# The first expert's token numbers from a one-column product, and what is queued behind its gathered rows

## The chip, the cores and the metric

One core of a Trainium2 chip runs the whole kernel in one launch. The metric is device time in microseconds (us), of one execution; the median of three runs stands for the kernel.

## The reference, cut to what matters

The kernel computes one step of a one-layer hybrid encoder over 576 tokens (512 of a prompt, 64 of a running stream) of 1024 features: a pooling mixer and a gated linear attention, a first layer norm that gives h, and then a routed mixture of experts on h with a second layer norm.

```python
logits = jnp.dot(x2, w_router) + b_router            # x2 = h, 576 x 1024; 32 experts
top_val, top_idx = lax.top_k(logits, TOP_K)          # 4 experts per token
gates = jax.nn.softmax(top_val, axis=-1)
...
gu = jnp.dot(xb, w_gu[e]) + b_gu[e]                  # xb: the rows of h routed to expert e
gate, up = gu[:, :EXPERT_FF], gu[:, EXPERT_FF:]
gate = jnp.minimum(gate, SWIGLU_LIMIT)
up = jnp.clip(up, -SWIGLU_LIMIT, SWIGLU_LIMIT)
hmid = gate * jax.nn.sigmoid(SWIGLU_ALPHA * gate) * (up + 1.0)
return jnp.dot(hmid, w_down[e]) + b_down[e]
...
y = _layer_norm(alpha * h + moe_out, ln2_g, ln2_b)
```

Each expert holds 12.6 MB of float32 weights: w_gu (8.4 MB) and w_down (4.2 MB). All 32 are read once.

## The kernel before, in words

The kernel is written by hand, one instruction list per engine, with counting semaphores between them; there is no planner. Each engine does its list in the order of the text.

**Two stages.** The first (some 228 us) makes h in five token tiles (four of 128 tokens, one of 64), stores h to DRAM from ACT's queue (L882), and routes each tile. The second loops over 32 experts, up to 96 tokens each.

**The weights.** `load(e, i, s)` (L515) brings piece i of expert e, 2 MB, into slot s of a ring of 8 slots in SBUF: pieces 0 to 3 are w_gu, 4 and 5 are w_down, below written (e, i). SP issues all of them in order. Ahead of the experts it issues (0,0) to (0,3), (1,0) and (1,1); then, after `mix_ready`, (0,4) and (0,5); then the gate and up biases (L532) once h is stored; then it waits for `gathered[0]`, the landing of expert 0's rows, and goes on with (1,2) and all others. Piece (e, i) waits for `split_done`, which says that the piece that was in its slot eight pieces earlier has been converted; piece (e, 1), whose slot held (e-2, 5), waits instead for `down_read`, the end of the last matmul of expert e-2. So (1,2) needs expert 0's pairs 0 and 1, and (2,1) needs the end of expert 0.

**The float16 pairs.** Float32 weights are multiplied as a high and a low half in float16. A piece is two "pairs" of 128 x 2048. For pair p of expert n, ACT writes the high half (`next_hi`, L871) and DVE the low one (`next_lo`, L1835, counted by `split_done`); PE multiplies both against the tokens' high and low halves. Pairs 0 to 3 are gate and up of the first half, 4 to 7 of the second, 8 and 9 the first half of w_down; the rest of w_down goes in float32. The four buffers come free by `unit_used`.

**Which tokens.** `rank` holds for every token its place in each expert. DVE's `onehot(m, e)` (L1765) compares the places with 0..127 and gives five 128 x 128 matrices `hot`. PE's `table(m, e)` multiplies them with `info`, four columns per expert: gate high, gate low, slot number, token number. DVE's `rows_of` copies the result to `found` (L1775) and makes the integer token numbers `tok_i` (L1777); POOL's `gather` (L684) then fetches those rows of h by an indirect DMA into `xg`. PE transposes them (`rows`, L1316), ACT and DVE make the halves (`rows_hi` L895, `rows_lo` L1826). A small product, `sel_ready`, picks the 96 slots out of 128, and `places_of` (L1783 to L1790) turns them into the scatter's addresses. The `table` product of expert 1 also counts the tokens of all experts, in float32.

**The seam between the stages.** For the last tile DVE does `route(4)` (the top four), then `gate_info(4)` (L1667 to L1674: softmax and the columns of `info`), `rank_tile(4)` (L1681), then `onehot(0)`, `rows_of(0)`, `onehot(1)`, `rows_of(1)`, two constants, the matrices `used` and `used16` (L1849 to L1852), the biases (L1853, `bias_ready`), `next_lo(0,0)`, `next_lo(0,1)`, `rows_lo(0)`, `places_of(0)`, `next_lo(0,2)` and on. PE fills its waits with products that nobody reads (`idle(n)`: n matmuls of 512 columns); they keep it active. POOL, after the last `pow` (L665), waits for all states and h rows to be stored, clears `xg` (L670), writes two index tables (L672, L674) that only the overflow loop reads, and gathers.

The queue order in SP's list around the change (L527 to L533):

```python
sp.wait_ge(mix_ready, TILES)
for i in (4, 5):
    load(0, i, piece_slot(0, i))
sp.wait_ge(hT_ready, 2 * TILES)
sp.wait_ge(h_stored, 16 * TILES)
sp.dma_start(bguT[:, 0:E, :], b_gu).then_inc(late_in, 16)
sp.wait_ge(gathered[0], 16)
```

Of the kernel before, what the change touches and what calls it, by code (L numbers as in the profile page):

```python
# [26 lines left out]
ALU = mybir.AluOpType  # L27
# [3 lines left out]
P = 128  # L31
# [4 lines left out]
TILES = 5  # L36
# [15 lines left out]
E = 32  # L52
TOPK = 4
FF = 1024
BLK = 96
# [18 lines left out]
def build(nc, x_prompt, x_sample, x_t, state_pool, state_gla, w_in, w_glr, w_pool, pool_scale, w_gate_up,  # L74
# [3 lines left out]
    with ExitStack() as ctx:  # L78
# [261 lines left out]
        acc_out, ln2_in = sem("acc_out"), sem("ln2_in")  # L340
# [127 lines left out]
        def _(sp):  # L468
# [58 lines left out]
            sp.wait_ge(mix_ready, TILES)  # L527
            for i in (4, 5):
                load(0, i, piece_slot(0, i))
            sp.wait_ge(hT_ready, 2 * TILES)  # L530
            sp.wait_ge(h_stored, 16 * TILES)
            sp.dma_start(bguT[:, 0:E, :], b_gu).then_inc(late_in, 16)  # L532
            sp.wait_ge(gathered[0], 16)  # L533
            for e in range(1, E):
                for i in range(2 if e == 1 else 0, PER):

                    if e == 2 and i == 0:
                        sp.dma_start(bd, b_down[0]).then_inc(bd_in, 16)
# [48 lines left out]
        def _(pool):  # L587
# [74 lines left out]
            for t in range(TILES):  # L662
# [4 lines left out]
            pool.wait_ge(states_out, 96)  # L667
            pool.wait_ge(h_stored, 16 * TILES)
            pool.wait_ge(mix_ready, TILES)
            step(pool.memset(xg, 0.0))  # L670
            pool.wait_ge(zeroed, 32)
            pool.iota(val_e, pattern=[[1, E], [0, MAXB - 1]], base=0, channel_multiplier=0,  # L672
                      allow_small_or_imprecise_dtypes=True).then_inc(made, 1)
            pool.iota(val_b, pattern=[[0, E], [BLK, MAXB - 1]], base=BLK, channel_multiplier=0,  # L674
                      allow_small_or_imprecise_dtypes=True).then_inc(made, 1)
# [25 lines left out]
            gather(0, 0, 0)  # L701
            gather(1, 1, 1)
# [302 lines left out]
        def _(pe):  # L1005
# [278 lines left out]
            idle(8)  # L1284

            def table(m, e):

                pe.wait_ge(hot_ready, m + 1)
# [13 lines left out]

            def rows(m, q, got, tables):
# [6 lines left out]
                mm(bank[0][0:BLK, 484:488], used16, found[m % ROW_BUFS if isinstance(m, int) else 0], True, True)\  # L1310
                    .then_inc(sel_ready, 1)
                pe.wait_ge(gathered[q], got)
                for b in range(2):
# [4 lines left out]
                    last.then_inc(gT_ready, 1)  # L1318

# [54 lines left out]
            idle(12)  # L1374
# [76 lines left out]
        def _(dve):  # L1451
# [208 lines left out]

            def gate_info(t):
# [7 lines left out]
                step(dve.tensor_tensor(each_g, each, g4.unsqueeze(2).to_broadcast([n, TOPK, E]), ALU.mult))  # L1669
                step(dve.tensor_reduce(gate, each_g.rearrange("p k e -> p e k"), AX.X, ALU.add))  # L1670
# [70 lines left out]
            dve.sem_inc(unit_used, BUFS)  # L1741
            route(TILES - 1)
            gate_info(TILES - 1)
            rank_tile(TILES - 1)
# [23 lines left out]
            def rows_of(m, q, last):  # L1768
# [4 lines left out]
                if isinstance(m, int) and m == 1:  # L1773
# [3 lines left out]
                dve.tensor_scalar(tok_i[q], found[q][:, 3:4], float(PLACES), None, ALU.add)\  # L1777
                   .then_inc(rows_known, 1)
# [69 lines left out]
            four = ident.rearrange("p (g d) -> p g d", d=4)  # L1848
            step(dve.tensor_copy(used[:, 0:BLK].rearrange("p (g d) -> p g d", d=3), four[:, :, 0:3]))  # L1849
            step(dve.tensor_copy(used[:, BLK:P].rearrange("p (g d) -> p g d", d=1), four[:, :, 3:4]))  # L1850
# [4 lines left out]
            next_lo(0, 0)  # L1855
            next_lo(0, 1)
            rows_lo(0, 0)
# [166 lines left out]
```

## Time and profile before

| | us |
|---|---|
| three runs, median (lowest to highest) | 1274.15 (1273.35 to 1274.99) |
| the profiled execution, own time | 1276.51 |
| its span in the profile | 1274.6 |
| PE busy | 1204.8 (95%) |
| DVE busy | 1050.7 (82%) |
| ACT busy | 945.0 (74%) |
| POOL busy | 176.3 (14%) |

Times in the rows below are microseconds from the start of the span, except where marked ns. PE is the matmul engine (TensorE), PEld its weight load, DVE VectorE, ACT ScalarE, POOL GpSimd, SP the engine that only issues DMAs; SPq and ACTq are their queues. A busy share is an average over stages: what a change in one stage is worth is read from that stage.

### The profile page before, as it was taken

The numbers are of one execution on the slowest core, as the hardware profiler recorded it, in microseconds if no ns is written. First come the engines' busy times: TensorE is split into PE (matmuls) and PEld (weight loads), VectorE is DVE, ScalarE is ACT, GpSimd is POOL, SyncE is SP. The second block draws the span as 40 slices with busy tenths as digits, with TensorE's granted clock in tenths as the row PEclk, the third lists the DMA queues.
The fourth block names the chain that finished last, engine by engine and source line by source line (L and its number), as shares of the span: only waits on it lengthen the run. The fifth ranks groups of instructions, "written<-read, shape, count | busy, mean of one in ns | idle before, by whom it ended". The sixth has DMA issues, their size and how long they took to land.

```text
span 1274.6 us, 35057 instructions
## 1 busy us (share of the span) xinstructions
PE 1204.8 (95%) x15390; PEld 872.2 (68%) x15390; DVE 1050.7 (82%) x1200; ACT 945.0 (74%) x1260; POOL 176.3 (14%) x145
## 2 busy tenths in 40 slices
PE   7999998799999999999999999999999999999985
PEld 3555555677777777777777777777777777777742
DVE  5565666899999889998988888888888888888877
ACT  5433311688989888988888888888888888888821
POOL 1264210111011100000000111111111111111002
PEclk9999997899999999999999999999999999999987
DMA  9562393599999999999999999999999999999982
GB/s 364 221 253 85 116 412 126 228 363 415 424 424 426 425 425 424 426 425 425 426 424 425 426 425 425 426 424 424 427 425 423 426 424 423 425 427 424 405 360 87
DMA packets 46839, 475.00 MB, mean 373 GB/s; under 512 B 8701, under 2 KB 9620, under 8 KB 20828
## 3 DMA queue, kind: packets, MB, share of 16 engines
q1 hardware_dynamic: 34636, 438.58, 82.2%
q0 software_dynamic: 11392, 31.77, 6.6%
q8 instruction: 124, 2.03, 0.6%
q10 hardware_dynamic: 656, 2.36, 0.5%
q14 instruction: 31, 0.25, 0.1%
HBM read 452.99 MB, written 29.95 MB: 379 GB/s over the span
## 4 chain that ended last, share of the span: by engine, by line
PE 34%; DMA 32%; DVE 9%; ACT 4%; issue 4%; DVEq 0%; ACTq 0%
PE wide L1007 23%; DMA ring<-in_w_gu 22%; PE bank L1007 9%; DMA ring<-in_w_down 8%; DVE work L1835 5%; ACT work L871 3%; DMA work<-part_rows 2%; PE bank L1316 1%; ACT work L901 1%; DVE ring L1967 1%; DVE ring L1965 1%; DVE work L1826 0%; DVE work L1765 0%; DVE ring L1954 0%; DVE work L1820 0%
## 5 line engine op out<-in xcount | busy, mean ns | idle before, releaser
L1835 DVE SCALAR_TENSOR_TENSOR work<-ring,work 128x2048 f16<-128x2048 f32 x320 | 721.3, 2287 | 109.7 <-ACT work L871 101.4
L871 ACT ACTIVATE work<-ring 128x2048 f16<-128x2048 f32 x320 | 599.6, 1902 | 93.9 <-DMA ring<-in_w_gu 67.1
L1007 PE MATMUL wide<-work 128*128 128x96 f16 (+2 forms) x7024 | 481.6, 229 | 34.6 <-issue 9.3
L1007 PEld LDWEIGHTS wide<-work 128*128 128x128 f16 (+2 forms) x7024 | 372.2, 101 | 129.0 <-issue 45.9
L1007 PEld LDWEIGHTS bank<-work 128*128 128x128 f16 (+4 forms) x6530 | 301.2, 101 | 39.7 <-issue 23.6
L1007 PE MATMUL wide<-ring,work 128*96 128x512 f32 (+3 forms) x1004 | 327.5, 493 | 0.0
L1007 PE MATMUL bank<-work 128*128 128x96 f16 (+4 forms) x6530 | 311.9, 208 | 9.2 <-DVE work L1765 3.6
L1007 PEld LDWEIGHTS wide<-ring,work 128*96 128x96 f32 (+3 forms) x1004 | 128.6, 134 | 172.7 <-issue 122.8
L684 POOL DMA_INDIRECT work<-h_rows,work x32 | 61.2, 1913 | 459.5 <-PE bank L1316 443.9
L697 POOL DMA_INDIRECT part_rows<-work x30 | 44.4, 1480 | 376.2 <-ACT work L931 376.2
L901 ACT ACTIVATE work<-wide,work 128x96 f32<-128x96 f32 x256 | 64.9, 333 | 0.0
L901 ACT ACTIVATE work<-bank,work 128x96 f32<-128x96 f32 x256 | 64.8, 333 | 0.0
L931 ACT ACTIVATE work<-wide,work 96x1024 f32<-96x1024 f32 x30 | 33.1, 1102 | 31.4 <-PE wide L1007 31.3
L910 ACT ACTIVATE work<-work 128x384 f32<-128x384 f32 x64 | 39.4, 616 | 2.1
L917 ACT ACTIVATE work<-work 128x384 f32<-128x384 f32 x64 | 39.4, 616 | 2.1
L863 ACT ACTIVATE work<-bank 128x512 f32<-128x512 f32 (+1 forms) x10 | 5.0, 553 | 44.5 <-PE bank L1234 44.5
L1815 DVE SCALAR_TENSOR_TENSOR work<-work 128x384 f32<-128x384 f32 x64 | 35.5, 555 | 1.3 <-DVE work L1805 0.2
L1458 DVE SCALAR_TENSOR_TENSOR ring<-ring 128x1024 f16<-128x1024 f32 x16 | 19.3, 1223 | 20.1 <-ACT ring L767 20.0
L1805 DVE SCALAR_TENSOR_TENSOR work<-work 128x384 f32<-128x384 f32 x64 | 35.2, 551 | 0.0
L1316 PE MATMUL bank<-work 128*128 128x128 f32 x256 | 34.5, 277 | 0.4 <-issue 0.4
L1826 DVE SCALAR_TENSOR_TENSOR work<-bank,work 128x384 f16<-128x384 f32 x64 | 32.5, 549 | 0.0
L895 ACT ACTIVATE work<-bank 128x384 f16<-128x384 f32 x64 | 27.3, 476 | 6.3 <-PE bank L1316 6.3
(205 smaller groups left out, 591.5 us busy)
## 6 DMA issues: line engine op xcount, KB each, us to landing
ring<-in_w_gu SPq DMA_DIRECT2D x128, 2048.0 KB, 30.1
ring<-in_w_down SPq DMA_DIRECT2D x64, 2048.0 KB, 33.2
part_rows<-work POOLq DMA_DIRECT2D x1, 10240.0 KB, 37.2
ring<-part_rows SPq DMA_DIRECT2D x3, 2560.0 KB, 27.5
ring<-in_w_in SPq DMA_DIRECT2D x3, 2048.0 KB, 13.2
ring<-in_w_out SPq DMA_DIRECT2D x2, 2048.0 KB, 10.5
h_rows<-work POOLq DMA_DIRECT2D x1, 2560.0 KB, 9.9
ring<-h_rows SPq DMA_DIRECT2D x1, 2560.0 KB, 23.2
```

The costliest lines, as they stand in the source:

```text
L684: pool.indirect_dma_start(xg, None, h_dram, bass.IndirectOffsetOnAxis(ap=tok_i[q], axis=0), bounds_check=PLACES - 1, oob_is_err=False)\
L697: pool.indirect_dma_start(part_dram, bass.IndirectOffsetOnAxis(ap=dst_i[p], axis=0), orow, None, bounds_check=TOPK * SPAN - 1, oob_is_err= ...
L871: act.activation(whi[buf(n, p)], packed(s, p), ACT.Copy, scale=W_UP).then_inc(hi_done, 1)
L901: last = act.activation(dst[:, c, :], b[:, c * BLK:(c + 1) * BLK], ACT.Relu, scale=-DOWN * S_UP, bias=bguT[:, at[0], at[1] + c:at[1] + c + 1])
L910: act.activation(sg, g1, ACT.Sigmoid, scale=-SWISH / S_UP, bias=sig_bias).then_inc(sig_done, 1)
L917: act.activation(u1, u1, ACT.Relu, scale=-1.0, bias=up_bias).then_inc(up_clip, 1)
L931: act.activation(orow, wide[1 if isinstance(n, int) else 0][0:BLK, :], ACT.Copy, scale=slots[p][:, 5:6])\
L1007: return pe.matmul(out, w, x, start=start, stop=stop, skip_group_check=True)
L1316: last = pe.transpose(bank[b][:, k * BLK:k * BLK + P], xg[:, (4 * b + k) * P:(4 * b + k + 1) * P], used)
L1805: dve.scalar_tensor_tensor(g1, g1, -LIMIT * S_UP, sg, ALU.add, ALU.mult).then_inc(gated, 1)
L1815: dve.scalar_tensor_tensor(hm[:, 4 * half:4 * half + 4, :], u1, (1.0 - LIMIT) * S_UP, g1, ALU.add, ALU.mult)\
L1835: dve.scalar_tensor_tensor(wlo[buf(n, p)], packed(s, p), W_UP, whi[buf(n, p)], ALU.mult, ALU.subtract).then_inc(split_done, 1)
```

## The change

It touches only the seam between the stages.

- SP: (0,4) and (0,5) are issued after the wait for `gathered[0]` instead of after `mix_ready`; the biases go ahead of them.
- POOL: `xg` is cleared as soon as `mix_ready` is there; the first gather waits for `h_stored` and its token numbers; the wait for the states and the two index tables come behind it.
- DVE: the two copies into `used` come ahead of `route(4)`. Then `first_hot` makes expert 0's one-hot matrices of tiles 0 to 3, `rank_tile(4)`, the fifth matrix, and `gate_info(4)`, in the midst of which `first_ids` turns the new product into token numbers. `onehot(0)` and the first `tok_i` of `rows_of` are gone. `next_lo(0,0)` comes ahead of the constants, `rows_lo(0)` ahead of `next_lo(0,1)`, and `used16` and the biases behind it.
- PE: after `positions(4)` three idle products instead of eight, then the one-column product (five matmuls, the token column of expert 0 alone), then four idle ones. Expert 0's select product goes behind the transposes and waits there for `bias_ready`. Twelve idle products ahead of `rows(0)` become six.

```diff
@@ SP
-            sp.wait_ge(mix_ready, TILES)
-            for i in (4, 5):
-                load(0, i, piece_slot(0, i))
             sp.wait_ge(hT_ready, 2 * TILES)
             sp.wait_ge(h_stored, 16 * TILES)
             sp.dma_start(bguT[:, 0:E, :], b_gu).then_inc(late_in, 16)
+            sp.wait_ge(mix_ready, TILES)
             sp.wait_ge(gathered[0], 16)
+            for i in (4, 5):
+                load(0, i, piece_slot(0, i))
@@ POOL
-            pool.wait_ge(states_out, 96)
-            pool.wait_ge(h_stored, 16 * TILES)
             pool.wait_ge(mix_ready, TILES)
             step(pool.memset(xg, 0.0))
-            pool.wait_ge(zeroed, 32)
-            pool.iota(val_e, ...)
-            pool.iota(val_b, ...)
+            pool.wait_ge(h_stored, 16 * TILES)
             gather(0, 0, 0)
+            pool.wait_ge(states_out, 96)
+            pool.wait_ge(zeroed, 32)
+            pool.iota(val_e, ...)
+            pool.iota(val_b, ...)
             gather(1, 1, 1)
@@ PE
             positions(TILES - 1)
-            idle(8)
+            idle(3)
+            pe.wait_ge(hot_ready, 1)
+            for t in range(TILES):
+                n = ROWS[t]
+                last = mm(bank[0][:, 488:489], hot[0:n, t, :], info[0:n, t, 0, 3:4], t == 0, t == TILES - 1)
+            last.then_inc(ids_ready, 1)
+            idle(4)
@@ PE, table
-                pe.wait_ge(hot_ready, m + 1)
+                pe.wait_ge(hot_ready, m + 2)
@@ PE, rows
                 if not isinstance(m, int) or m > 0:
                     pe.wait_ge(dst_known, m)
-                else:
-                    pe.wait_ge(bias_ready, 1)
-                mm(bank[0][0:BLK, 484:488], used16, found[...], True, True).then_inc(sel_ready, 1)
+                    select(m)
                 pe.wait_ge(gathered[q], got)
                 ... the eight transposes ...
+                if isinstance(m, int) and m == 0:
+                    pe.wait_ge(bias_ready, 1)
+                    select(m)
@@ PE
             table(0, 0)
             table(1, 1)
-            idle(12)
+            idle(6)
             rows(0, 0, 16, 2)
@@ DVE
+            def first_hot(tiles):
+                for t in tiles:
+                    n = ROWS[t]
+                    last = dve.tensor_scalar(hot[0:n, t, :], iota16[0:n, :], rank[0:n, t, 0:1], None, ALU.is_equal)
+                return last
+            def first_ids():
+                dve.wait_ge(ids_ready, 1)
+                dve.tensor_scalar(tok_i[0], bank[0][:, 488:489], float(PLACES), None, ALU.add).then_inc(rows_known, 1)
@@ DVE, gate_info, behind the product with the gates
+                if t + 1 == TILES:
+                    first_ids()
@@ DVE
+            step(dve.tensor_copy(used[:, 0:BLK]..., four[:, :, 0:3]))
+            step(dve.tensor_copy(used[:, BLK:P]..., four[:, :, 3:4]))
             route(TILES - 1)
+            first_hot(range(TILES - 1))
+            rank_tile(TILES - 1)
+            first_hot([TILES - 1]).then_inc(hot_ready, 1)
             gate_info(TILES - 1)
-            rank_tile(TILES - 1)
+            dve.nop().then_inc(hot_ready, 1)
@@ DVE, rows_of
+                if not isinstance(m, int) or m > 0:
                     dve.tensor_scalar(tok_i[q], ...).then_inc(rows_known, 1)
@@ DVE
-            onehot(0, 0)
             rows_of(0, 0, None)
             onehot(1, 1)
             rows_of(1, 1, None)
+            next_lo(0, 0)
             step(dve.memset(sig_bias, SWISH * LIMIT))
             step(dve.memset(up_bias, 2 * LIMIT * S_UP))
-            ... the two copies into used ...
+            rows_lo(0, 0)
+            next_lo(0, 1)
             dve.wait_ge(late_in, 16)
             step(dve.tensor_copy(used16, used[:, 0:BLK]))
             dve.tensor_scalar(bguT[:, 0:E, :], ...).then_inc(bias_ready, 1)
-            next_lo(0, 0)
-            next_lo(0, 1)
-            rows_lo(0, 0)
             places_of(0, 0)
             next_lo(0, 2)
```

## Rows read from the trace of the kernel before

**Rows 1.** The page's part 4, the chain that ended last, by engine.
```profile
PE 34%; DMA 32%; DVE 9%; ACT 4%; issue 4%; DVEq 0%; ACTq 0%
```

**Rows 2.** Busy time by stretch: PE, PEld, DVE, ACT, POOL, then PEclk, DMA share, GB/s.
```profile
240.00:271.00 31.00, 28.90 (x436) 22.79 (x437) 29.75 (x36) 25.64 (x33) 3.82 (x2) 1.00 0.94 359
271.00:274.00 3.00, 3.00 (x49) 2.17 (x48) 3.00 (x2) 1.11 (x1) 0.00 (x0) 1.00 0.56 135
274.00:277.00 3.00, 3.00 (x75) 3.00 (x73) 2.12 (x7) 2.54 (x2) 1.09 (x1) 1.00 0.85 333
277.00:1191.00 914.00, 888.29 (x13010) 685.65 (x13007) 803.76 (x828) 793.05 (x1015) 100.17 (x59) 1.00 1.01 425
```

**Rows 3.** Timeline of SP's queue: start, duration, instruction, count.
```profile
240.69 6.06 SPq L515 DMA_DIRECT2D ring<-in_w_gu  x2
...
272.28 0.80 SPq L515 DMA_DIRECT2D ring<-in_w_gu  x2
```

**Rows 4.** Timeline of DVE through the seam; in brackets idle time before, and releaser.
```profile
225.71 0.15 DVE L1667 RECIPROCAL work<-work 64x1 f32<-64x1 f32 x1 [0.35 <-ACT work L888]
...
226.48 0.37 DVE L1670 TENSOR_REDUCE work<-work 64x32 f32<-64x128 f32 x1
...
227.63 0.18 DVE L1681 SCALAR_TENSOR_TENSOR work<-wide,work 64x32 f32<-64x32 f32 x1
227.97 1.83 DVE L1765 TENSOR_SCALAR work<-work 128x128 f16<-128x128 f16 x5
...
230.45 0.15 DVE L1777 TENSOR_SCALAR work<-work 128x1 int32<-128x1 f16 x1
230.52 0.89 DVE L1765 TENSOR_SCALAR work<-work 128x128 f16<-128x128 f16 x5
...
234.73 0.15 DVE L1777 TENSOR_SCALAR work<-work 128x1 int32<-128x1 f16 x1
...
236.12 4.49 DVE L1835 SCALAR_TENSOR_TENSOR work<-ring,work 128x2048 f16<-128x2048 f32 x2
...
241.90 4.50 DVE L1835 SCALAR_TENSOR_TENSOR work<-ring,work 128x2048 f16<-128x2048 f32 x2
```

**Rows 5.** Timeline of PE through the seam.
```profile
229.86 0.36 PE L1007 MATMUL bank<-work 128*128 128x4 f16 x5 [2.31 <-DVE work L1765]
231.47 2.80 PE L1007 MATMUL bank<-work 128*128 128x32 f32 x15 [1.25 <-DVE work L1765]
234.20 4.12 PE L1007 MATMUL wide<-work 128*128 128x512 f16 x12
...
238.18 1.07 PE L1316 MATMUL bank<-work 128*128 128x128 f32 x8
241.59 8.52 PE L1007 MATMUL bank<-work 128*128 128x96 f16 x197 [2.34 <-DVE work L1826]
```

**Rows 6.** Timeline of POOL, and the first two gathers' times from issue to landing.
```profile
228.10 1.01 POOL L670 MEMSET work<- 128x1024 f32 x1 [8.90 <-issue]
...
231.49 1.18 POOL L684 DMA_INDIRECT work<-h_rows,work  x1 [1.23 <-DVE work L1777]
...
DMA to landing us min/median/max: 3.6/6.9/10.2
```

**Rows 7.** Timeline of ACT: rows' high halves, then the first pairs' that wait for PE.
```profile
238.85 0.93 ACT L895 ACTIVATE work<-bank 128x384 f16<-128x384 f32 x2 [6.33 <-PE bank L1316]
243.93 3.87 ACT L871 ACTIVATE work<-ring 128x2048 f16<-128x2048 f32 x2 [4.15 <-PE bank L1007]
```

**Rows 8.** Stretches with TensorE's granted clock; columns as in Rows 2.
```profile
226.70:230.10 3.40, 1.09 (x9) 0.42 (x7) 2.81 (x10) 3.37 (x4) 1.92 (x3) 1.00 0.33 88
230.10:237.00 6.90, 5.65 (x24) 3.63 (x24) 3.53 (x17) 2.42 (x2) 1.34 (x2) 0.51 0.17 48
```

**Rows 9.** Groups of instructions running between 294.3 and 295.1: count, busy us, mean ns.
```profile
L1835 DVE SCALAR_TENSOR_TENSOR work<-ring,work 128x2048 f16<-128x2048 f32 x1 | 2.3, 2286 | 0.0
...
L707 POOL IOTA work<- 96x580 f32 x1 | 0.7, 657 | 0.0
```

More of the change, by code:

```diff
@@ L339, in build @@
         ov_place = sem("ov_place")
-        acc_out, ln2_in = sem("acc_out"), sem("ln2_in")
+        ids_ready, ln2_in = sem("ids_ready"), sem("ln2_in")
         y_done, y_stored = sem("y_done"), sem("y_stored")
@@ L701, in _ @@
             gather(0, 0, 0)
+            pool.wait_ge(states_out, 96)
+            pool.wait_ge(zeroed, 32)
+            pool.iota(val_e, pattern=[[1, E], [0, MAXB - 1]], base=0, channel_multiplier=0,
+                      allow_small_or_imprecise_dtypes=True).then_inc(made, 1)
+            pool.iota(val_b, pattern=[[0, E], [BLK, MAXB - 1]], base=BLK, channel_multiplier=0,
+                      allow_small_or_imprecise_dtypes=True).then_inc(made, 1)
             gather(1, 1, 1)
@@ L1301, in table, with select @@
                 last.then_inc(table_ready, 1)
+            def select(m):
+                mm(bank[0][0:BLK, 484:488], used16, found[m % ROW_BUFS if isinstance(m, int) else 0], True, True)\
+                    .then_inc(sel_ready, 1)
             def rows(m, q, got, tables):
@@ L1307, in rows @@
                     pe.wait_ge(dst_known, m)
-                else:
-                    pe.wait_ge(bias_ready, 1)
-                mm(bank[0][0:BLK, 484:488], used16, found[m % ROW_BUFS if isinstance(m, int) else 0], True, True)\
-                    .then_inc(sel_ready, 1)
+                    select(m)
                 pe.wait_ge(gathered[q], got)
@@ L1741, in _ @@
             dve.sem_inc(unit_used, BUFS)
+            four = ident.rearrange("p (g d) -> p g d", d=4)
+            step(dve.tensor_copy(used[:, 0:BLK].rearrange("p (g d) -> p g d", d=3), four[:, :, 0:3]))
+            step(dve.tensor_copy(used[:, BLK:P].rearrange("p (g d) -> p g d", d=1), four[:, :, 3:4]))
             route(TILES - 1)
+            first_hot(range(TILES - 1))
+            rank_tile(TILES - 1)
+            first_hot([TILES - 1]).then_inc(hot_ready, 1)
             gate_info(TILES - 1)
-            rank_tile(TILES - 1)
+            dve.nop().then_inc(hot_ready, 1)
             def counts():
@@ L1776, in rows_of @@
                 dve.wait_ge(table_copied, m + 1)
-                dve.tensor_scalar(tok_i[q], found[q][:, 3:4], float(PLACES), None, ALU.add)\
-                   .then_inc(rows_known, 1)
+                if not isinstance(m, int) or m > 0:
+                    dve.tensor_scalar(tok_i[q], found[q][:, 3:4], float(PLACES), None, ALU.add)\
+                       .then_inc(rows_known, 1)
             def places_of(m, q):
@@ L1844, in _ @@
             rows_of(1, 1, None)
+            next_lo(0, 0)
             step(dve.memset(sig_bias, SWISH * LIMIT))
             step(dve.memset(up_bias, 2 * LIMIT * S_UP))
-            four = ident.rearrange("p (g d) -> p g d", d=4)
-            step(dve.tensor_copy(used[:, 0:BLK].rearrange("p (g d) -> p g d", d=3), four[:, :, 0:3]))
-            step(dve.tensor_copy(used[:, BLK:P].rearrange("p (g d) -> p g d", d=1), four[:, :, 3:4]))
+            rows_lo(0, 0)
+            next_lo(0, 1)
             dve.wait_ge(late_in, 16)
```

4 lines of the change are left out of this document (removed).

## The prediction

> **What bounds the kernel now.** I read the chain of waits first, and it misleads. It lays 34% of the span on PE and 32% on DMA [rows 1], as if two engines shared the bound. The busy times by stretch correct it: from 277 to 1191 us, 914 us, the DMA share is 1.01 and the rate 425 GB/s [rows 2], with no slack anywhere between. The chain follows a weight piece back to whatever released its issue; it does not see that the piece then stood in a full queue. So nearly all of the span is one stream of weights, and its end moves with the time at which it last ran dry. That place is in rows 2 as well: from 240 to 271 the share is 0.94 at 359 GB/s, from 271 to 274 it is 0.56 at 135 GB/s, and after that it never falls again. What ends the hole is the issue of (2,1) and (2,2) at 272.28 [rows 3]. (2,1) needs the last matmul of expert 0 (`down_read`), so **expert 0's end sets the restart of the stream, and the restart sets the end of the kernel**. The seam counts in two ways only: when expert 0 ends, and whether the pieces ahead of (2,1) are through by then.
>
> **Token numbers and gather.** Before, DVE does the gate columns (225.71 on), ranks tile 4 at 227.63, compares until 229.80, PE multiplies, and the numbers are there at 230.45 + 0.15 = 230.60 [rows 4]. After: DVE is free of `route(4)` at 225.36 (0.35 ahead of 225.71). Four compares take 0.72, by the 0.89 for five at 230.52; the rank step takes 227.97 - 227.63 = 0.34; the fifth compare 0.18: 226.60. The five one-column matmuls are seen by DVE 0.40 after they may start (an estimate: the table of 229.86 took 0.36 [rows 5]): 227.06. DVE meanwhile does the first three gate steps, 226.48 - 225.71 = 0.77, until 227.37, and adds: 227.52, **3.1 earlier**. The gather started 231.49 - 230.60 = 0.89 behind its numbers and landed 3.6 after its start [rows 6], at 235.1; after: 228.4 and 232.0. Its other wait, h stored, was over when POOL began at 228.10 [rows 6] with 4 MB beside that store; without them it is no later. The two copies into `used` go into DVE's wait for the last logits; if that cover were gone they would cost 0.4.
>
> **Expert 1's table.** The rest of the gates, 227.63 - 226.48 = 1.15, runs until 228.7, and expert 0's table is copied by 229.3. The compares for expert 1 then take 0.89, or up to 1.83 where POOL writes beside them: those at 227.97 ran beside the clearing and the index tables at 228.10 and took twice as long [rows 4, 6]. The two tables now start at 228.4 + 1.18 = 229.6, in the middle of the compares; I take 1.3, until 230.6. From the end of the compares (231.41) to the end of `rows_of(1)` (234.88) it was 3.47 [rows 4]: **234.1, 0.8 earlier**. Of the 3.1 the gather gains, 2.3 are spent, on the longer way of DVE.
>
> **To expert 0's start.** PE: the idle products start 234.20 - 231.47 = 2.73 behind the table [rows 5], at 233.4, and six at up to 0.43 (the 12 took 4.12 with the last at full clock) end at 236.0; the rows have been there since 232.0. Transposes then, and ACT begins 238.85 - 238.18 = 0.67 later [rows 5, 7] and hands DVE its first half at 237.15. DVE: `next_lo(0,0)` 2.2 (half of the 4.4 that two take from start to start), two constants 0.2, until 236.5; it waits for 237.15; `rows_lo` 0.93 to 238.1; `next_lo(0,1)` to 240.3; `used16` and biases 0.6 (half of the 236.12 - 234.88 = 1.24 that they, the constants and the copies took [rows 4]) to 240.9. Only here may PE take the select product and, behind it, expert 0's first matmul: 241.0 against 241.59 [rows 5]. DVE waits 0.4 for the select, spends 0.45 on the addresses (0.93 and 0.45 are what 241.90 - 236.12 = 5.78 leaves beside the 4.4) and starts `next_lo(0,2)` at 241.75 **against 241.90** [rows 4].
>
> From there DVE has no idle time until expert 0's last pairs, and its work is unchanged: expert 0 ends with DVE. Its end is therefore **0.15 earlier**, 272.1. The new wait on `bias_ready` on PE is what makes it so little: behind it stands all of expert 0, and ahead of it the whole second pair.
>
> **The stream ahead of (2,1).** 240 to 274 carried 31 x 0.359 + 3 x 0.135 = 11.5 MB [rows 2]. (0,4) and (0,5) add 4.2, so 15.7 MB less what of it is behind (2,1)'s issue, some 0.3: 15.4. At 425 GB/s that is 36.3 us. Issued at 232.1, with 1 to 1.5 until data flow, they are through at 269.7 to 270; at the 0.359 that the stretch had before, taken for the five old pieces alone, at 232.1 + 1 + 9.9 + 31 = 274. I take the first, nearer since two pieces always stand in the queue now. Then the stream is dry at (2,1) as before and follows expert 0's end. At the second it joins without a hole, at about the time (274.1 by the 277 less what 3 us at 333 GB/s had fallen short of 425) that the old one was at full rate: no loss. The step that I put at nothing, two pieces out of an idle stretch into a full one (9.9 us of transfer), is so covered by 8.6 us of earlier issue and by the hole. If expert 0 ended before 270, they would cost.
>
> **Sum.** -0.15 at expert 0's end, and -0.2 for a hole that gets a little shorter: -0.35. Against the profiled execution, 1276.51, that is 1276.2; it stands 2.4 above the median of 1274.15, and with the same difference the forecast is **1273.8**. What a measurement of this kernel can tell is about 0.2%, 2.5 us.
>
> **A rule against the change.** Beside an index table of POOL at 294.4 a low-half conversion of DVE took 2286 ns [rows 9], as those at 236.12 and 241.90 do without one [rows 4]. This bears on the clearing of `xg`, which now runs at 219.2, right after the last `pow` and beside h's last operation on DVE, which leads the chain; I cost it at nothing. The Trainium skill, "GPSIMD Engine Reference", section "Specifications", says that VectorE and GpSimd contend when the DVE instruction uses a two-port mode or has two SBUF inputs. By that rule the conversion should have been slowed too (both inputs are in SBUF), and h's last operation would be. The compares agree with it, the conversion does not.
>
> **Rivals.**
> 1. *The clock stays up.* PEclk falls near 230.1, after a stretch with PE busy 1.09 of 3.4, and is 0.51 until 237 [rows 8]: 1.2 in place of 2.4 GHz. After the change four idle products and a table stand in that stretch, some 1.7. If this holds 2.4 GHz, the table of expert 1 and six idle products take half: 1.2 less to `rows_of(1)` and 2.4 less to the transposes. Then DVE waits for nothing: 1.6 less at `next_lo(0,2)`, **1272.3**. Against it: 1.7 is still half idle.
> 2. *That, and the stream joins.* With expert 0's end at 270.4 and the pieces through at 270 to 271.5, the hole closes too, 1.2 more: **1271.0**. Needs both.
> 3. *The clock is down at expert 0's start; slower.* Between transposes and select, 237.1 to 241.0, PE now has nothing, 3.9 us against 2.3 before 241.59 [rows 5]; before 229.86 an idle 2.31 and 1.25 more went with the fall. Its place is the first pairs of expert 0. At 2.4 GHz PE needs 8.52/197 x 48 = 2.1 for a pair [rows 5], under DVE's 2.2; at 1.2 GHz 4.2. One slow pair (243.93 + 1.6) is hidden, as DVE comes to pair 4 only at 247. Two end at 249.6, ACT's conversion (1.9 each [rows 7]) at 251.5, and DVE wants it at 249.1: +2.4, and some more behind: **1276.8**. It decides if 1.2 GHz lasts past about 247. The Trainium skill, "TensorE: Matmul & The Clock Gate", section "What's actually happening", has the clock set by how busy PE has lately been; by it both this and rival 1 are open.
> 4. *The port rule holds for h's last operation:* it grows by up to 1.0, the length of the clearing [rows 6], and all behind it: +1.0, **1274.8**.
> 5. *The gather lands no earlier* (indirect DMA issue or h's store late). Up to 236.0 the stream is through by 274.1 and nothing changes; behind that each us costs one.
>
> **How the numbers follow.** My forecast 0.46, rival 1 0.17, rival 2 0.13, rival 3 0.14, rivals 4 and 5 0.10. Faster by over 0.2% are rival 2 and a tail of rival 1: 0.17. Slower are rival 3 and a tail of 4 and 5: 0.15. The range takes in rivals 1 and 4, most of 2, the bounds of the idle products and of the compares (0.5 each), and goes to just short of rival 3, with 0.8 for the scatter of the runs: 1271.2 to 1276.5.
>
> **What the profile would show.** `tok_i` near 227.5, the gather at 228.4 and landing by 232; `rows_of(1)` done near 234.1; PE's first 96-column matmul near 241.0 behind a gap of nearly 4 us; `next_lo(0,2)` within 0.3 of 241.9; SP's (2,1) within 0.5 of 272.3 with a dip in the rate there; then 425 GB/s to the end. It is wrong if PEclk is 1.0 over 230 to 237 or 0.5 behind 243, if h is done later, or if the dip at 272 is gone.

## The result and the profile after

| | before | after |
|---|---|---|
| median, 20 runs each (lowest to highest), us | 1274.2 (1271.3 to 1277.4) | 1278.35 (1274.6 to 1281.1) |
| ratio, 95% interval | | 1.0032 (1.0023 to 1.0042) |
| the profiled execution: own time, span | 1276.51, 1274.6 | 1274.57, 1272.7 |
| mean granted clock, share of 2.4 GHz | 0.984 (138 runs) | 0.981 (20 runs) |

The changed kernel is slower by 4.1 us, above my range (1271.2 to 1276.5). The profiled execution of after is its shortest, that of before lies above its median, so the two spans stand the wrong way round. They must be compared from a common mark. I take the end of `route(4)` on DVE: 225.36 before (0.35 ahead of 225.71 [rows 4]), 222.17 + 0.37 = 222.54 after. It falls anywhere between 222.0 and 226.0 in the profiles below, whichever kernel they are of.

One part of the change lies ahead of this mark and costs 0.4 us there, which no number counted from the mark holds: the two copies into `used`. DVE before, then after, from the rank step of the tile ahead:

```profile
222.60 0.19 DVE L1681 SCALAR_TENSOR_TENSOR work<-bank,work 128x32 f32<-128x32 f32 x1
223.46 0.18 DVE L1649 TENSOR_TENSOR work<-bank,work 64x32 f32<-64x32 f32 x1 [0.66 <-PE bank L1007]
```

```profile
219.36 0.19 DVE L1708 SCALAR_TENSOR_TENSOR work<-bank,work 128x32 f32<-128x32 f32 x1
220.17 0.21 DVE L1771 COPY work<-work 128x96 f32<-128x96 f32 x1 [0.61 <-DVE work L1708]
...
220.64 0.18 DVE L1662 TENSOR_TENSOR work<-bank,work 64x32 f32<-64x32 f32 x1
```

The copies start only behind the idle 0.61 that was to cover them. From the end of the rank step to the mark it is 225.36 - 222.79 = 2.57 before and 222.54 - 219.55 = 2.99 after; it is 2.98 to 3.08 in all twelve profiles with the copies there and 2.52 to 2.93 in the six without.

The seam on DVE after (start, duration, instruction; in brackets idle time ahead of it and its releaser), answering to rows 4:

```profile
222.17 0.37 DVE L1671 TENSOR_REDUCE work<-work 64x32 f32<-64x128 f32 x1
...
224.48 0.16 DVE L1684 TENSOR_SCALAR work<-bank 128x1 int32<-128x1 f32 x1
...
226.37 1.60 DVE L1799 TENSOR_SCALAR work<-work 128x128 f16<-128x128 f16 x5
...
231.28 0.15 DVE L1812 TENSOR_SCALAR work<-work 128x1 int32<-128x1 f16 x1
231.37 2.29 DVE L1870 SCALAR_TENSOR_TENSOR work<-ring,work 128x2048 f16<-128x2048 f32 x1
...
234.96 1.02 DVE L1861 SCALAR_TENSOR_TENSOR work<-bank,work 128x384 f16<-128x384 f32 x2 [1.15 <-ACT work L896]
...
239.55 4.49 DVE L1870 SCALAR_TENSOR_TENSOR work<-ring,work 128x2048 f16<-128x2048 f32 x2
...
247.71 2.29 DVE L1870 SCALAR_TENSOR_TENSOR work<-ring,work 128x2048 f16<-128x2048 f32 x1 [0.43 <-ACT work L872]
...
251.08 4.49 DVE L1870 SCALAR_TENSOR_TENSOR work<-ring,work 128x2048 f16<-128x2048 f32 x2 [0.61 <-ACT work L872]
```

POOL's clearing and gather (answering to rows 6):

```profile
215.91 0.94 POOL L669 MEMSET work<- 128x1024 f32 x1
225.61 1.17 POOL L679 DMA_INDIRECT work<-h_rows,work  x1 [8.75 <-DVE work L1684]
```

PE (rows 5), then ACT (rows 7):

```profile
228.02 2.80 PE L1008 MATMUL bank<-work 128*128 128x32 f32 x15 [1.89 <-DVE work L1799]
230.75 2.74 PE L1008 MATMUL wide<-work 128*128 128x512 f16 x6
233.29 1.48 PE L1326 MATMUL bank<-work 128*128 128x128 f32 x8
238.82 11.17 PE L1008 MATMUL bank<-work 128*96 128x4 f16 x198 [4.05 <-DVE work L1886]
```

```profile
234.37 0.93 ACT L896 ACTIVATE work<-bank 128x384 f16<-128x384 f32 x2 [5.09 <-PE bank L1326]
243.04 1.91 ACT L872 ACTIVATE work<-ring 128x2048 f16<-128x2048 f32 x1 [7.75 <-PE bank L1008]
245.76 1.91 ACT L872 ACTIVATE work<-ring 128x2048 f16<-128x2048 f32 x1 [0.81 <-PE bank L1008]
```

What the change meant to do, it did: the gather starts 3.07 behind the end of `route(4)`, against 6.13. But PE stands idle for 4.05 us ahead of expert 0, and then its first 198 matmuls take 11.17 us, where 197 took 8.52 [rows 5]. The stretches show why (columns as in rows 2; after the comma PE busy, and the third number from the right is PEclk). After:

```profile
234.00:237.40 3.40, 0.77 (x6) 0.53 (x4) 2.44 (x3) 0.93 (x2) 1.04 (x1) 0.97 1.04 443
237.40:240.80 3.40, 1.98 (x25) 1.98 (x26) 3.00 (x8) 0.00 (x0) 0.00 (x0) 0.53 0.95 407
240.80:244.20 3.40, 3.40 (x46) 3.40 (x44) 3.40 (x4) 1.16 (x1) 0.00 (x0) 0.50 1.05 440
244.20:247.60 3.40, 3.40 (x81) 3.40 (x79) 2.94 (x6) 2.59 (x3) 0.00 (x0) 0.97 1.00 424
```

Before, over its first pairs:

```profile
238.20:241.60 3.40, 1.06 (x11) 0.82 (x9) 3.40 (x5) 0.93 (x2) 1.38 (x1) 1.00 0.00 0
241.60:245.00 3.40, 3.40 (x80) 3.40 (x81) 3.37 (x6) 1.07 (x1) 0.00 (x0) 1.00 0.98 323
```

After a stretch in which PE worked 0.77 of 3.4 us the clock fell to 1.2 GHz, near 237.6, and it came back near 244.4; 46 matmuls went through where before 80 did. ACT's conversions for pairs 4 and 5 wait for PE to free a buffer (7.75 and 0.81), and DVE waits for ACT (0.43, 0.61). Expert 0 ends late, and the stream restarts late. SP's queue and the stretches around the restart (rows 3 and 2):

```profile
229.46 0.81 SPq L515 DMA_DIRECT2D ring<-in_w_down  x2
238.21 6.20 SPq L515 DMA_DIRECT2D ring<-in_w_gu  x2
```

```profile
271.38 2.65 SPq L515 DMA_DIRECT2D ring<-in_w_gu  x3
```

```profile
268.00:271.00 3.00, 3.00 (x8) 1.08 (x7) 3.00 (x2) 1.50 (x1) 0.00 (x0) 1.00 0.59 243
271.00:274.00 3.00, 3.00 (x68) 2.81 (x67) 3.00 (x5) 1.62 (x2) 0.59 (x1) 1.00 0.61 153
274.00:277.00 3.00, 3.00 (x75) 3.00 (x73) 2.13 (x5) 2.93 (x2) 0.51 (x1) 1.00 0.97 415
277.00:1189.00 912.00, 886.34 (x12983) 684.31 (x12980) 803.13 (x828) 790.44 (x1014) 92.64 (x59) 1.00 1.01 424
```

From the end of `route(4)` to the issue of (2,1): 272.28 - 225.36 = 46.9 before, 271.38 - 222.54 = 48.8 after, **1.9 later**. The hole in the stream now takes in two of these stretches, and behind it the rate is 424 GB/s to the end (425 before).

The end of the kernel has a clock of its own. Its last stage, behind the stream, ends with 44 float32 products; before, then after (timeline of PE):

```profile
1246.39 15.78 PE L1007 MATMUL wide<-work 116*116 116x512 f32 x44 [1.98 <-DMA work<-part_rows]
```

```profile
1246.14 14.09 PE L1008 MATMUL wide<-work 116*116 116x512 f32 x44 [1.54 <-DMA work<-part_rows]
```

From the mark they start at 1021.03 before and at 1023.60 after, 2.6 us later, and with the 0.4 ahead of the mark 3.0. Then they take 1.7 less, with a mean granted clock of 0.87 behind 1240 against 0.80. No edit touches that stage, and b_swap (14.09) and b_swap2 (15.78), one and the same kernel, differ in the same way: it is luck, and it hides 1.7 us of the loss in this pair of profiles.

### The profile page after: what moved, and what is told of

The parts are those of the page before. It is cut to its first block, busy times and chain, and to the rows that moved or that the text cites. A ratio compares the mean times of both kernels' runs of the same rounds, so it can differ in the third digit from the quotient of the medians.

```text
span 1272.7 us, 35055 instructions
## 1 busy us (share of the span) xinstructions
PE 1202.8 (95%) x15388; PEld 874.0 (69%) x15388; DVE 1051.0 (83%) x1200; ACT 944.2 (74%) x1260; POOL 168.0 (13%) x145
## 4 chain that ended last, share of the span: by engine, by line
PE 57%; DMA 24%; DVE 10%; ACT 4%; issue 4%; POOL 0%; DVEq 0%; SPq 0%; ACTq 0%
PE wide L1008 39%; PE bank L1008 17%; DMA ring<-in_w_gu 16%; DMA ring<-in_w_down 6%; DVE work L1870 4%; ACT work L872 3%; DMA work<-part_rows 2%; PE bank L1326 1%; ACT work L902 1%; DVE ring L1997 1%; DVE ring L1995 1%; DMA ring<-in_x_t 0%; DVE ring L1984 0%; DVE work L1861 0%; DVE work L1855 0%
## 5 line engine op out<-in xcount | busy, mean ns | idle before, releaser
L1008 PEld LDWEIGHTS bank<-work 128*128 128x128 f16 (+2 forms) x6535 | 304.0, 101 | 41.0 <-issue 24.3
L1008 PE MATMUL bank<-work 128*128 128x96 f16 (+3 forms) x6535 | 314.8, 209 | 9.7 <-DVE work L1886 4.1
L679 POOL DMA_INDIRECT work<-h_rows,work x32 | 55.4, 1733 | 481.8 <-PE bank L1326 457.2
```

What stands on the lines that cost most here:

```text
L679: pool.indirect_dma_start(xg, None, h_dram, bass.IndirectOffsetOnAxis(ap=tok_i[q], axis=0), bounds_check=PLACES - 1, oob_is_err=False)\
L1008: return pe.matmul(out, w, x, start=start, stop=stop, skip_group_check=True)
```

## The experiments

Sixteen measurements were made, in four groups: thirteen edits, two of them twice, and the changed kernel once more. Each has 11 or 12 runs, and the kernel before 33 to 35 beside them on the same chip. "Clock" is the mean granted clock over its runs (the kernel before: 0.984 to 0.985 in every group). The last two columns are of the one profiled execution, from the end of `route(4)`: the start of `next_lo(0,2)`, and the end of expert 0 (the start of ACT's weighing of its output, L931 before).

| kernel | median us | before | ratio (95%) | clock | next_lo(0,2) | expert 0 ends |
|---|---|---|---|---|---|---|
| before | | | | 0.984 | 16.5 | 46.9 |
| after (20 runs) | 1278.35 | 1274.2 | 1.0032 (1.0023 to 1.0042) | 0.981 | 17.0 | 48.9 |
| after_again | 1277.44 | 1275.89 | 1.0021 (1.0007 to 1.0035) | 0.982 | 17.1 | 49.1 |
| a_fill | 1275.44 | 1274.35 | 1.0004 (0.9993 to 1.0016) | 0.985 | 17.0 | 47.4 |
| a_sp_back | 1276.68 | 1274.35 | 1.0016 (1.0004 to 1.0028) | 0.982 | 16.3 | 48.1 |
| a_sp_back2 | 1276.3 | 1275.89 | 1.0019 (1.0005 to 1.0033) | 0.982 | 17.0 | 48.9 |
| a_units_first | 1277.0 | 1274.35 | 1.0017 (1.0006 to 1.0028) | 0.984 | 17.0 | 47.4 |
| b_no_idle | 1275.45 | 1274.35 | 1.0009 (0.9994 to 1.0024) | 0.981 | 16.1 | 47.3 |
| b_sp_only | 1274.36 | 1275.7 | 0.9991 (0.9980 to 1.0002) | 0.985 | 15.5 | 45.9 |
| b_reorder | 1277.86 | 1275.7 | 1.0015 (1.0006 to 1.0025) | 0.981 | 16.6 | 48.4 |
| b_ids | 1273.41 | 1275.89 | 0.9997 (0.9982 to 1.0011) | 0.984 | 16.7 | 47.1 |
| a_bias_early | 1275.29 | 1275.37 | 0.9988 (0.9973 to 1.0003) | 0.985 | 15.5 | 45.9 |
| a_warm | 1274.16 | 1275.7 | 0.9991 (0.9981 to 1.0000) | 0.987 | 14.8 | 46.4 |
| b_swap | 1274.12 | 1275.7 | 0.9985 (0.9975 to 0.9994) | 0.985 | 15.0 | 45.4 |
| b_swap2 | 1274.43 | 1275.37 | 0.9989 (0.9977 to 1.0002) | 0.984 | 16.8 | 47.2 |
| a_warm_swap | 1273.79 | 1275.89 | 0.9997 (0.9982 to 1.0012) | 0.987 | 14.8 | 46.4 |
| b_sp_swap | 1271.92 | 1275.37 | 0.9984 (0.9971 to 0.9996) | 0.985 | 15.4 | 45.8 |
| a_best | 1273.01 | 1275.37 | 0.9984 (0.9972 to 0.9996) | 0.986 | 14.4 | 44.8 |

Two theories. **Clock**: PE's wait for the biases leaves it idle, its clock falls, expert 0's first pairs run at 1.2 GHz, and expert 0 ends late. **Stream**: (0,4) and (0,5) stand in the way of the pieces behind them.

### a_fill: keep PE busy in the gap

```diff
                 if isinstance(m, int) and m == 0:
+                    flat = info.rearrange("p t e c -> p (t e c)")
+                    for _ in range(10):
+                        mm(wide[1][:, 512:1024], flat[:, 0:P], flat[:, 0:512], True, True)
                     pe.wait_ge(bias_ready, 1)
                     select(m)
```

> The changed kernel with ten matmuls of 512 columns that nobody reads, put on PE between expert 0's transposes and its wait for the biases. Clock theory (PE is idle for 4 us ahead of expert 0, the granted clock falls to 1.2 GHz, expert 0's first pairs run at it and its end is 2 to 4 us late): PEclk is 1.0 over the first pairs, and the kernel comes back to 1272.5 to 1275, near the kernel before. Stream theory ((0,4) and (0,5) stand in the way of the pieces behind them): no change from the changed kernel, 1277 to 1279.

Measured: 1275.44, ratio 1.0004, where after had 1.0032 and 1.0021. The wait, the new order and SP's list are all still there; only the ten products that nobody reads were added. Its stretches, the timeline of PE, and of ACT:

```profile
234.00:237.40 3.40, 2.78 (x15) 1.32 (x13) 2.61 (x3) 0.95 (x2) 1.04 (x1) 0.99 1.02 439
237.40:240.80 3.40, 2.15 (x50) 2.16 (x51) 3.03 (x8) 0.00 (x0) 0.00 (x0) 1.00 0.97 417
240.80:244.20 3.40, 3.40 (x85) 3.40 (x82) 3.40 (x5) 3.08 (x2) 0.00 (x0) 1.00 1.06 442
```

```profile
234.46 2.32 PE L1008 MATMUL wide<-work 128*128 128x512 f16 x10
238.65 8.61 PE L1008 MATMUL bank<-work 128*96 128x4 f16 x198 [1.87 <-DVE work L1889]
```

```profile
241.07 3.87 ACT L872 ACTIVATE work<-ring 128x2048 f16<-128x2048 f32 x2 [5.92 <-PE bank L1008]
```

The clock is 0.99 to 1.00 in these stretches, the 198 matmuls take 8.61 instead of 11.17, and ACT does pairs 4 and 5 without a break. `next_lo(0,2)` stands at 17.0 as in after, and expert 0 ends 1.5 us sooner (47.4 against 48.9). With only unread products added, the low clock is the cause of this 1.5. By the times a_fill is clear of after (from 1.0023 up), but its interval overlaps that of after_again (from 1.0007 up); how much of the whole loss the clock makes is less sure than that it makes a part.

### a_sp_back, twice: SP's order of before in the changed kernel

```diff
+            sp.wait_ge(mix_ready, TILES)
+            for i in (4, 5):
+                load(0, i, piece_slot(0, i))
             ...
-            sp.wait_ge(mix_ready, TILES)
             sp.wait_ge(gathered[0], 16)
-            for i in (4, 5):
-                load(0, i, piece_slot(0, i))
```

> The changed kernel with SP's order of before: (0,4) and (0,5) issued after mix_ready. Clock theory: 1277 to 1279, as the changed kernel, perhaps 0.5 less. Stream theory: about 4 us are given back, 1273.5 to 1275.

> The same kernel as a_sp_back (SP's order of before in the changed kernel), again. Clock theory: within 1 us of after_again. If the order of SP costs where expert 0 ends late, 1.5 us or more under after_again, as the first runs hinted (1276.7 against 1278.4).

> The changed kernel once more, unedited, beside the others of this call, so that each of them can be set against it on the same chip. 3 to 4.5 us slower than the kernel before; mean granted clock near 0.981 against 0.984; low clock over expert 0's first pairs in the profile.

Measured: 1.0016 the first time; the second time 1.0019 beside 1.0021 of after_again on the same chip. after_again was expected 3 to 4.5 us slower than before and was 1.6 slower by the medians, 2.7 by the ratio. The clock stays low (0.982). SP's order is not where the loss is; what the first runs hinted did not repeat.

### b_sp_only and b_reorder: one part of the change alone

b_sp_only is the kernel before with SP's order of after. b_reorder is the kernel before with the new order of DVE, the late select product and six idle products:

```diff
-            step(dve.tensor_copy(used[:, 0:BLK]...)) ; step(dve.tensor_copy(used[:, BLK:P]...))
-            dve.wait_ge(late_in, 16) ; used16 ; biases -> bias_ready
-            next_lo(0, 0) ; next_lo(0, 1) ; rows_lo(0, 0)
+            next_lo(0, 0) ; constants ; rows_lo(0, 0) ; next_lo(0, 1)
+            dve.wait_ge(late_in, 16) ; used16 ; biases -> bias_ready
```

> The kernel before with SP's order of after and nothing else: (0,4) and (0,5) behind expert 0's gathered rows. The gather is as late as before (landing near 235), so the two pieces start near 235.5 and the pieces ahead of (2,1) are through near 273 to 274. Clock theory: the clock has nothing to do with it; -0.5 to +0.7 to the kernel before, 1273.7 to 1275. Stream theory: the whole cost is here, 1277 to 1279.

> The kernel before with the new order of DVE and PE alone (used made early, next_lo(0,0), constants, rows_lo, next_lo(0,1), biases; select product and its wait for the biases behind the transposes; six idle products instead of twelve); no one-column product, SP as before. Clock theory: the wait on PE comes with this part, so the cost comes with it: low clock over expert 0's first pairs, mean granted clock near 0.981 to 0.982, 1276.5 to 1279. Stream theory: no cost, 1274 to 1275.

Measured: b_sp_only 0.9991, no cost at all and if anything a gain; b_reorder 1.0015, clock 0.981. The loss comes with the new order behind `rows_of(1)`, the wait in it, and without the one-column product or SP's order. b_reorder's stretches over its first pairs:

```profile
240.40:243.80 3.40, 2.18 (x28) 2.19 (x29) 3.00 (x8) 0.00 (x0) 0.00 (x0) 0.50 0.74 216
243.80:247.20 3.40, 3.40 (x47) 3.40 (x46) 3.40 (x5) 1.36 (x1) 0.00 (x0) 0.52 0.97 414
```

### b_ids: the one-column product alone

The changed kernel with SP's order, the order behind `rows_of(1)`, the early select product and twelve idle products of before.

> The changed kernel with only the one-column product kept (with POOL's new order): SP as before, DVE's order after rows_of(1) as before (biases, both pairs, rows_lo), the select product ahead of the transposes, twelve idle products. Clock theory: no wait for the biases behind the transposes, so expert 0's first pairs mostly run at 2.4 GHz: -1 to +0.5 to the kernel before, mean granted clock 0.984. If the cost is in the product or in POOL's order, +2 to +4.

Measured: ratio 0.9997, clock 0.984. The product and POOL's new order cost nothing that can be measured. They also gain nothing: the gather starts 3.6 behind `route(4)` instead of 6.1, and `next_lo(0,2)` stands at 16.7 as before.

### b_no_idle: the gap in the kernel before

```diff
-            idle(12)
             rows(0, 0, 16, 2)
```

> The kernel before without its twelve idle products ahead of expert 0's transposes, and nothing else changed. The transposes come about 3 us earlier, and PE then waits some 5 us for the first pair, as DVE is no earlier. Clock theory: expert 0's first pairs run at 1.2 GHz, PEclk near 0.5 over some 7 us there, and the kernel is 2 to 5 us slower than before, 1276 to 1279. Stream theory: as before, 1273.5 to 1275.

Measured: clock 0.981, as expected, but ratio 1.0009, not 1.0015 or more, over the widest scatter of all (1271.0 to 1280.4). Half a miss. In its profile the clock was back near 244.7, 3.0 us into expert 0 (near 244.4 and 5.6 us in after), and expert 0 took 31.1 from `next_lo(0,2)` on, 0.7 more than in before. As I read it, fewer matmuls are slow and more of them lie within what hides the first slow pair; that was not tried by itself.

### a_units_first: the wait behind the first pair

```diff
                 for u in range(8):
                     unit(n, u, n % 2)
+                    if n == 0 and u == 1:
+                        pe.wait_ge(bias_ready, 1)
+                        select(0)
```

> The changed kernel with expert 0's select product and its wait for the biases moved behind expert 0's first two units (its first pair), so that PE begins as soon as the rows' halves are there, some 3 us earlier. Clock theory: the gap on PE ahead of expert 0 shrinks to some 1.5 us, the first pairs run at 2.4 GHz more often, 1272 to 1274.5. Stream theory: as the changed kernel, 1277 to 1279.

Measured: ratio 1.0017. The clock came back as expected (0.984), expert 0 ends at 47.4 in its profile as in a_fill, but the time did not come back. There is no contradiction with a_fill in this: `next_lo(0,2)` is 0.5 later than in before, and the copies cost 0.4 ahead of the mark, in both kernels. These 0.9 us are a ratio of 1.0007, which lies in both intervals. Whether the rest of the 1.0017 is scatter stays open.

### a_bias_early: the wait shortened

```diff
+            dve.wait_ge(late_in, 16) ; used16 ; biases -> bias_ready
             rows_lo(0, 0)
             next_lo(0, 1)
-            dve.wait_ge(late_in, 16) ; used16 ; biases -> bias_ready
```

and PE waits for the rows' low halves too ahead of the select product, which shares their bank.

> The changed kernel with used16 and the biases made ahead of rows_lo(0) and next_lo(0,1) instead of behind them. In the changed kernel's profile DVE is idle 1.15 us there, so they cost next to nothing, and PE's gap ahead of expert 0 shrinks from 4.05 us to some 1.5. If that wait is the cause: mean granted clock 0.984 or more, next_lo(0,2) at 16.4 behind the end of route(4) instead of 17.0, and 0 to 1 us faster than the kernel before. If the cause is elsewhere in the new order: as the changed kernel, +2 to +4.

Measured: 0.9988, as expected; at most 1.0003, so clear of after and of after_again. The biases fill DVE's idle 1.15 (timeline of DVE, then of PE):

```profile
237.43 0.43 DVE L1885 TENSOR_SCALAR work<-work 128x512 f32<-128x512 f32 x1
237.84 1.02 DVE L1862 SCALAR_TENSOR_TENSOR work<-bank,work 128x384 f16<-128x384 f32 x2
...
241.43 4.49 DVE L1871 SCALAR_TENSOR_TENSOR work<-ring,work 128x2048 f16<-128x2048 f32 x2
```

```profile
239.01 4.37 PE L1008 MATMUL bank<-work 128*96 128x4 f16 x97 [1.29 <-DVE work L1862]
```

PE's gap is 1.29, and `next_lo(0,2)` starts 241.43 - 225.89 = 15.5 behind `route(4)`, where 16.4 was expected. So this edit does two things at once: expert 0 runs at full clock, and DVE, which no longer has the biases and the wait for the select product in its way, is 1.5 earlier. Some 0.5 of that is the clock over the transposes (1.08 against 1.48 in after). It shows that the order of the biases was the fault, and does not by itself tell the clock from the longer way of DVE; a_fill does.

### a_warm, b_swap twice, a_warm_swap, b_sp_swap, a_best: how much is to be had

a_warm puts six idle products behind the one-column product, six between the tables and fourteen ahead of the wait. b_swap is the kernel before with

```diff
-                for i in range(2 if e == 1 else 0, PER):
+                for i in (range(2, PER) if e == 1 else (0, 2, 1, 3, 4, 5) if e == 2 else range(PER)):
```

a_warm_swap and b_sp_swap put that edit into a_warm and b_sp_only; a_best is a_bias_early with it and six idle products in each of three gaps.

> The changed kernel with idle products in every gap of PE through the seam: six instead of four behind the one-column product, six between the two tables, fourteen between transposes and the wait for the biases. Clock theory: the clock stays at 2.4 GHz from the last tile to expert 0 in most executions, the table of expert 1 takes 1.8 instead of 2.8, the transposes come some 2 us earlier, and what the gather gained arrives: 1271.5 to 1273.5, mean granted clock 0.986 or more. Stream theory: 1277 to 1279, as the changed kernel.

> The kernel before with (2,2) issued ahead of (2,1). If the end of the kernel hangs on when the weight stream last ran dry, at (2,1) behind expert 0's end, then (2,2), whose slot comes free some 2 us earlier, fills part of that hole, and the kernel is 1 to 2 us faster, 1272.3 to 1273.5. If PE sets the end there, or the hole's bytes don't count, no change, 1274.3.

> The same kernel as b_swap, again: 1 to 2.5 us faster than the kernel before if the gain is real, within 0.7 if it was scatter.

> a_warm (idle products in every gap of PE through the seam) with (2,2) issued ahead of (2,1), as in b_swap. If the two gains are of different places (clock at expert 0's start; the hole in the weight stream), they add up: 2 to 3 us faster than the kernel before, mean granted clock near 0.987. If b_swap's gain was another thing's, as a_warm, about 1 us faster.

> The kernel before with both edits of SP's list: (0,4) and (0,5) behind the gathered rows, and (2,2) ahead of (2,1). Both act on the same hole in the stream, so they don't add up: 1 to 2 us faster than the kernel before, as either alone. If b_sp_only's gain came from another place (h's store no longer beside 4 MB of weights), they add up to 3 us.

> a_bias_early with idle products in the gaps of PE (six behind the one-column product, six between the tables, six behind the transposes) and (2,2) ahead of (2,1). next_lo(0,2) near 14.4 behind the end of route(4), against 16.5 before; expert 0 ends 1 to 2 us earlier, the hole in the stream is filled: 2 to 3.5 us faster than the kernel before.

Measured, a_warm: the clock holds (0.987), the table of expert 1 takes 1.71 instead of 2.80, and `next_lo(0,2)` is at 14.8. Only 1.5 us of the median came of it (ratio 0.9991, just reaching 1). Its profile shows one reason, a stop in the midst of expert 1's transposes that no engine released (timeline of PE):

```profile
231.10 1.71 PE L1008 MATMUL bank<-work 128*128 128x32 f32 x15 [0.49 <-DVE work L1803]
```

```profile
259.08 0.77 PE L1326 MATMUL bank<-work 128*128 128x128 f32 x5 [1.45 <-issue]
```

The same stop, 1.42 us, is in a_warm_swap. A table at full clock in one profile proves little by itself: it takes 1.71 in b_swap's too, where the seam is that of before, and that is why `next_lo(0,2)` is at 15.0 there and at 16.8 in b_swap2, the same kernel. b_swap: (2,2) goes out at 268.67, and the hole is filled (SP's timeline, then the stretch):

```profile
268.67 4.73 SPq L515 DMA_DIRECT2D ring<-in_w_gu  x3
```

```profile
271.00:274.00 3.00, 3.00 (x76) 3.00 (x73) 2.93 (x6) 2.01 (x2) 1.11 (x1) 1.00 0.96 404
```

Before it was 135 GB/s [rows 2]. Ratios 0.9985 and 0.9989, the second just reaching 1: likely a gain of about 1.5 us. b_sp_only fills the same hole, with its two late pieces:

```profile
271.00:274.00 3.00, 3.00 (x75) 3.00 (x73) 2.12 (x3) 2.93 (x4) 0.00 (x0) 1.00 1.01 399
```

The combinations, b_sp_swap (0.9984) and a_best (0.9984), are 2.4 to 3.5 us under the kernel before by their medians and beat both kernels. Their parts do not add up measurably: in a_best expert 0 ends 2.2 us earlier than before, and it is no faster than b_sp_swap. Why is not shown. Its profile shows one part: the last float32 products start at 1018.4 from the mark, 1.9 ahead of b_sp_swap's, and then take 17.24 where b_sp_swap's take 14.09. a_warm_swap was a miss: 0.9997; its last products start at 1018.9 and take 17.15. Whether the clock falls there more often when the stage starts earlier was not tried.

**All runs together.** Over the 346 runs, each kernel with its own level, the time rises by 0.31 us (standard error 0.014) for each us at 1.2 GHz (that time being twice the span by one minus its mean granted clock). The 20 runs of after have 0.003 less clock than before: 8 us more at 1.2 GHz, and so 2.5 us of time, if the slope holds for the seam too: it is taken over low clock anywhere in the kernel, the last stage included.

## Why the prediction was wrong

**What bounds the kernel: right as far as is shown.** Behind the restart the stream is full in after as in before (424 and 425 GB/s), and over the 18 profiles the start of the last float32 products follows the end of expert 0 (correlation 0.90, both from the mark). That closing the hole without touching an engine makes the kernel faster is likely (b_swap, b_swap2), though a_warm_swap does not show it. What the prediction left out is the last stage, whose own clock is worth 1.7 to 3.2 us in single executions.

**Token numbers and gather: right.** Predicted 2.2 from the end of `route(4)` to the numbers (227.52 - 225.36) and the gather's start at 3.0; measured 224.64 - 222.54 = 2.1 and 3.07. `rows_of(1)` was put at 8.7 and ended at 8.9.

**Ahead of the mark: 0.4 put at nothing.** "The two copies into `used` go into DVE's wait for the last logits": they stand behind that wait, not in it, and the text's own price for that, 0.4, is what they cost.

**To expert 0's start: mis-sized by 0.6.** `next_lo(0,2)` was put 0.15 earlier than before; it is 17.01 against 16.54 behind the mark, 0.47 later. The transposes were priced at full clock; they ran partly at 1.2 GHz and took 1.48, not 1.07, and ACT began 1.08 behind them, not 0.67. DVE waited 1.15 for it, where I had 0.65.

**From there to expert 0's end: this step failed.** "DVE has no idle time until expert 0's last pairs, and its work is unchanged" took the clock for granted. From `next_lo(0,2)` to expert 0's end it takes 30.4 us in before, a_fill, a_units_first, b_ids, b_swap, b_swap2, b_sp_only, b_sp_swap, a_bias_early and a_best, and 31.7 to 32.0 in after, after_again, a_sp_back, a_sp_back2 and b_reorder: 1.3 to 1.6 more, in waits of DVE for ACT, and of ACT for PE at 1.2 GHz. The text had named the gap of nearly 4 us, named the clock's fall as rival 3 with its place, and gave it 0.14. The kernel before already showed such a fall at 230.1, behind a stretch in which PE was busy 1.09 of 3.4 us, and the planned gap left PE with less work than that. This likeness should have given rival 3 far more than 0.14. It is no rule: from 238.2 to 241.6 of the same kernel PE is busy 1.06 of 3.4, and there the clock held. Rival 3's price of 2.4 for two slow pairs was too high: they cost 1.5 in this profile, and with the 0.5 ahead of them that makes the 1.9 by which the restart is late.

**The rest.** In the profiled pair 0.4 (copies), 0.5 (start of expert 0), 1.5 (its slow pairs) and some 0.6 behind the restart, whose cause is open, make 3.0 of the 4.1 us. The five profiles with after's wait end expert 0 at 48.1 to 49.1, mean 48.7; the five with before's order of DVE and PE (before, b_sp_only, b_swap, b_swap2, b_sp_swap) at 45.4 to 47.2, mean 46.2: 2.4 us. The two measured losses are 4.1 and 1.6 by the medians, 4.1 and 2.7 by the ratios, so that a third of the first may be scatter; which of the two is nearer is open.

**The stream ahead of (2,1): later than predicted, and without harm.** It was to be through near 270, 44.6 behind the mark. The rate over 268 to 271 of after, 243 GB/s, puts it near 269.7 there, and with the mark at 222.54 that is 47.2, between the text's two bounds (44.3 and 48.6). As expert 0 ended late too, a hole was left all the same. That the two pieces cost nothing is shown by b_sp_only (0.9991) and by a_sp_back2 beside after_again (1.0019 and 1.0021).

**Clearing `xg` beside h's last operation: right at nothing.** The clearing, 215.91 to 216.85, ran beside the first half of the last operation, whose two halves took 1.41 after as before: no sign of the contention that the Trainium skill ("GPSIMD Engine Reference", "Specifications") gives for two SBUF inputs. The compares were slowed again, 1.60 beside the gather and the index tables against 0.89. They have one SBUF input, so the page would cover them only by its other case, the two-port mode, and no run here shows in which mode they ran.

**Rivals 1 and 2** did not happen in the changed kernel, but a_warm and a_best show that the clock can be held up, by idle products in the gaps (0.987 and 0.986). The price of rival 2 did not come: a_best ends expert 0 at 44.8 behind the mark, where the rival had 45.0, and measured 1273.0, not 1271.0.

## What to carry to other kernels

A wait of some microseconds put on the matmul engine can cost more than itself: look at what it leaves of the engine's activity, and at the granted clock in the stretch where the next real work begins. Before moving work behind a wait, look for an idle hole on the engine that has to produce what is waited for; here 0.6 us of bias work fitted into an idle 1.15 and removed the whole loss. Where a full DMA queue sets the end, find the last place where it ran dry: reordering two loads there was likely worth some 1.5 us, as much as the work on the engines around it. And when two single profiles are compared, put the common mark ahead of everything that was changed, and look behind the last changed place for differences that no edit made.

## What the runs showed of the hardware

The granted clock fell to 1.2 GHz although PE worked through 0.77 us of the 3.4 before, and stayed there for 5.6 us of unbroken 96-column matmuls, 46 in 3.4 us against 80 to 85. In the kernel before it held behind 3.4 us with 1.06 of work and fell behind 3.4 us with 1.09. Executions of one kernel differ by up to 9.4 us, and over half of that variance goes with how long each had spent at 1.2 GHz (correlation 0.81 over the 20 runs of after). The last 44 float32 products take 14.09, 15.78 or some 17 us in the profiles, with no edit near them. A stop of 1.4 us on PE that no engine released appeared at the same instruction in a_warm and a_warm_swap, the two kernels with fourteen idle products ahead of expert 0; what it is, was not tried.
